# First mixer of a fused two-block kernel: where GpSimd builds its second rotation table, and where two state-space sums stand on TensorE

## The reference, cut to what matters

```python
z = hn @ hy_w_in[i]
y_a = rwkv7_time_mix(z[..., :RWKV_COLS], ...)
y_b = s5_ssm(z[..., RWKV_COLS:], ...)
y_mix = jnp.concatenate([y_a, y_b], axis=-1) @ hy_w_out[i]

def s5_ssm(u, lam_re, lam_im, ...):
    lam_bar = jnp.exp(lam * dt)
    bu = jnp.einsum('gpi,btgi->btgp', b_bar, ug)
    _, states = lax.associative_scan(combine, (lam_bar, bu), axis=1)
    y = jnp.real(jnp.einsum('gip,btgp->btgi', c_mat, states))
    y = y + d_skip * ug
    ...

def rwkv7_recurrence(r, decay, k, v, kk, a):
    def step(state, inp):
        s_kk = jnp.einsum('bhvk,bhk->bhv', state, kk_t)
        state = state * w_t - s_kk[..., None] * (kk_t * a_t) + v_t[..., None] * k_t
        return state, jnp.einsum('bhvk,bhk->bhv', state, r_t)
```

## Time and profile before

| | us |
|---|---|
| median of 3 runs | 2951.21 |
| lowest and highest | 2950.44, 2955.02 |
| the profiled execution | 2949.55 |
| its span | 2947.7 |
| first mixer's part of the span that the change touches | 54 to 244 |
| TensorE busy from 109 to 190 | 51.45 of 81.00 |
| TensorE busy from 190 to 256 | 44.82 of 66.00 |
| TensorE busy over the whole span | 2784.8 (94%) |

### The profile page before, as it was taken

One profiled execution on the slowest core, in us unless ns is written; L12 is line 12 of the kernel. 1 busy time (PEld: TensorE's weight loads), 2 busy tenths in 40 slices (PEclk: granted clock), 3 DMA queues, 4 the chain that ended last, 5 costly groups with the idle time before them and its releaser, 6 DMA issues.

```text
span 2947.7 us, 44095 instructions
## 1 busy us (share of the span) xinstructions
PE 2784.8 (94%) x18634; PEld 2478.1 (84%) x18634; DVE 2129.6 (72%) x2071; ACT 1701.7 (58%) x1770; POOL 118.0 (4%) x112
## 2 busy tenths in 40 slices
PE   8558999999799999999999999999999899999999
PEld 6447899998798878888887888888887799989999
DVE  7864545556545888888888888888888666766676
ACT  6203544346554677767776777676777564445543
POOL 5541000000000000000000000000000000000000
PEclk9888999999899999999999999999999999999999
DMA  6002435553243999899999999999999545544453
GB/s 225 30 2 73 133 126 172 185 172 116 72 161 143 352 347 359 340 354 343 354 342 349 353 354 355 344 351 350 349 356 349 215 145 168 183 132 144 158 186 129
DMA packets 238003, 690.42 MB, mean 234 GB/s; under 512 B 10608, under 2 KB 169456, under 8 KB 178416
## 3 DMA queue, kind: packets, MB, share of 16 engines
q1 hardware_dynamic: 235728, 685.52, 64.6%
q10 hardware_dynamic: 2080, 2.10, 0.2%
HBM read 686.53 MB, written 1.05 MB: 233 GB/s over the span
## 4 chain that ended last, share of the span: by engine, by line
PE 70%; DVE 9%; DMA 8%; issue 5%; ACT 4%; POOLq 2%; POOL 2%; DVEq 1%; ACTq 0%; SPq 0%
PE ps L800 20%; PE ps L802 20%; PE ps L801 20%; DMA ring<-moe 7%; DVE w_lo L3463 2%; DVE more_lo L3463 2%; PE ps L1633 1%; PE ps L860 1%; ACT arena L1766 1%; PE ps L1685 1%; DVE w_lo L1817 1%; DMA ring<-w_in 1%; PE ps L1082 1%; ACT w_hi L1801 1%; DVE mix L2588 1%
## 5 line engine op out<-in xcount | busy, mean ns | idle before, releaser
L1817 DVE TENSOR_TENSOR w_lo<-ring,w_hi 128x1024 fp32r<-128x1024 f32 x362 | 446.8, 1247 | 354.4 <-ACT w_hi L1801 353.2
L1801 ACT ACTIVATE w_hi<-ring 128x1024 fp32r<-128x1024 f32 x362 | 381.1, 1058 | 424.7 <-PE ps L802 403.9
L800 PE MATMUL ps<-x_hi,w_hi 128*128 128x256 f32 x1952 | 559.5, 287 | 13.2 <-DVE x_lo L2988 7.1
L801 PE MATMUL ps<-x_lo,w_hi 128*128 128x256 f32 x1952 | 553.7, 284 | 0.0
L802 PE MATMUL ps<-x_hi,w_lo 128*128 128x256 f32 x1952 | 553.6, 284 | 0.0
L1769 ACT ACTIVATE w_hi<-ring 128x2048 fp32r<-128x2048 f32 x232 | 445.3, 1920 | 181.8 <-DMA ring<-moe 169.6
L3463 DVE TENSOR_TENSOR w_lo<-ring,w_hi 128x2048 fp32r<-128x2048 f32 x232 | 523.4, 2286 | 16.1 <-ACT w_hi L1769 14.6
L800 PEld LDWEIGHTS ps<-x_hi,w_hi 128*128 128x128 f32 x1952 | 375.5, 192 | 21.7 <-issue 13.7
L801 PEld LDWEIGHTS ps<-x_lo,w_hi 128*128 128x128 f32 x1952 | 375.8, 193 | 0.3
L802 PEld LDWEIGHTS ps<-x_hi,w_lo 128*128 128x128 f32 x1952 | 375.7, 192 | 0.0
L1769 ACT ACTIVATE more_hi<-ring 128x2048 fp32r<-128x2048 f32 x115 | 220.7, 1919 | 133.2 <-DMA ring<-moe 127.7
(11 more groups left out here) (392 smaller groups left out, 5034.0 us busy)
## 6 DMA issues: line engine op xcount, KB each, us to landing
ring<-moe SPq DMA_DIRECT2D x347, 1024.0 KB, 6.7
more_raw<-moe SPq DMA_DIRECT2D x115, 1024.0 KB, 6.9
ring<-ffn_w_up SPq DMA_DIRECT2D x44, 1024.0 KB, 5.1
ring<-ffn_w_down SPq DMA_DIRECT2D x22, 1024.0 KB, 4.9
ring<-xa_w_kv SPq DMA_DIRECT2D x16, 1024.0 KB, 5.4
ring<-w_in SPq DMA_DIRECT2D x16, 1024.0 KB, 6.8
ring<-da_w_qkv SPq DMA_DIRECT2D x12, 1024.0 KB, 5.2
ring<-ff_w_gate SPq DMA_DIRECT2D x11, 1024.0 KB, 5.3
```

What stands on the lines that cost most here:

```text
L800: mm(o, lhs[0], rhs[0], start=start, stop=False)
L801: mm(o, lhs[0], rhs[1], start=False, stop=False)
L1801: nc.scalar.activation(w_hi[:, half_slot(at, half), :], ring[:, s_, half * 1024:half * 1024 + 1024], ACT.Copy).then_inc(hi_ready, 1)
L1817: nc.vector.tensor_tensor(w_lo[:, i, :], ring[:, s_, half * 1024:half * 1024 + 1024], w_hi[:, i, :], ALU.subtract).then_inc(lo_ready, 1)
```

## The change

Two places are edited, both orders of calls. On TensorE, `s5_sum(4)` moves from ahead of `level(3)` to behind it, and `s5_sum(5)` from ahead of `s5_drive(6)` and `level(4)` to behind both. On GpSimd, `table(1)` moves from behind `s5_out(0)` to ahead of it. No instruction is added or taken away, and every wait stays with its instruction.

```diff
@@ TensorE, pe_first_mixer
             s5_drive(5)
+            level(3)
             s5_sum(4)
-            level(3)
-            s5_sum(5)
             s5_drive(6)
             level(4)
+            s5_sum(5)
             s5_drive(7)
@@ GpSimd, pool_first_mixer
             table(0, s5_pair(0, 2))
+            table(1, s5_pair(0, 2))
             s5_out(0)
-            table(1, s5_pair(0, 2))
             s5_out(1)
```

## The result

The changed kernel takes 2935.73 us in the median of 6 runs (2932.87 to 2938.84). The kernel before, run beside it, takes 2950.82 (2945.98 to 2955.02). The ratio is 0.995 with a 95% interval of 0.9938 to 0.9962, so 15 us are gained, between 11 and 18. The forecast was 2936.5 with a gain of 14.7. The profiled execution takes 2933.28 with a span of 2931.5; before it was 2949.55 and 2947.7. Ratios and their intervals are given here as they are on record. They are not the quotients of the two medians, and a gain taken from the one can differ from the other by some 4 us.

The account below looks back on a forecast made before the run. Engines waiting in turn for one another in the first mixer were the winnable bound, the expert stage being full; 14.1 us from the levels plus 0.6 from the table took 2951.2 to 2936.5 us, range 2932 to 2941.

Parts of the forecast that it names:

- Level 3: TensorE's level 3 in the first mixer starts once add_level(2) is done, at 190.15 in place of 195.26.
- The cold clock: Level 3 starts at half clock after TensorE's idle time: 1.6 us extra, from 1.1 us a group over one and a half.
- The bound of 3.3: Upper bound on level 3's half-clock cost, with all three matmul groups cold: 3.3 us.
- Level 4's add and L1246: VectorE is free for level 4's add at 209.7; TensorE's next step, L1246, starts at 212.1, 14.1 us earlier.
- Behind L1246: The chain after the levels keeps its waits and lengths, so all of it moves by 14.1 us.
- Behind the mixer: Later stages, including the expert stage, keep their lengths, so the gain was taken in full through to the end.
- The early table: table(1) moved ahead of s5_out(0): saves 10.9 us late, delays VectorE some 10.2 us early; net gain 0.6 us.
- The rival of a TensorE that loses more than its slack: Early stall makes TensorE's chunks 5 to 8 exceed four microseconds of slack by some 5 us: 2941.5 us; chance 0.10.
- The open choice: Whether VectorE's L2565 form and a copy are blocked beside GpSimd; taken as blocked, otherwise 2.9 us less delay.
- The rival of the free table: VectorE wins its turns beside table 1 between 55 and 71, gaining 10.9 us in full: 2926.2 us; chance 0.12.
- The given-back: Levels' gain lost to GpSimd's late piece 5 or to later stages: within 2 us of before, 2950; chance 0.07.
- the slower rival: TensorE's clock stays half after its new idle stretch at 61 to 70: 19 us slower, 2970 us; chance 0.03.

Follow-up runs that it names:

- e4: Changed kernel with table(1) back behind s5_out(0), its temporary in a place of its own, operands waiting for table 0 only; 2932.96 us in one run.
- e1: Kernel before with only the two sums moved behind the levels, GpSimd's order as before; 2932.1 us against 2950.12, ratio 0.9951.
- e3: Changed kernel with table(1) left out, two zero-filling memsets in its place, so it computes something else; 2924.72 us in one run.
- e5: Changed kernel with table(1) behind s5_out(1), its temporary in s5_x, operands waiting for table 0 alone; 2933.01 us in one run.
- e2: Kernel before with only table(1) moved early, the sums as before; 2943.94 us against 2950.12, ratio 0.9983.
- e6: Changed kernel with s5_sum(5) put back ahead of s5_drive(6) and level(4), so only s5_sum(4) is moved; 2944.49 us in one run.
- e9: The kernel of e2 run a second time; 2949.25 us against 2948.39 for the kernel before, ratio 0.9999.
- e7: Changed kernel with s5_sum(1), s5_sum(6) and s5_sum(7) also moved behind the steps they stood ahead of; 2936.38 us against 2948.39, ratio 0.9951.
- e8: Changed kernel with add_level(2) ahead of s5_scan(4) on VectorE and sums 6 and 7 moved later; 2930.2 us against 2949.67, ratio 0.9921.

## Why the prediction was right, point by point

- **Level 3** was to start at 190.15 and did at 189.18; with the table half's 0.93 taken off that is exact. The cold clock was put at 1.6 us, and it was 3.68 - 2.08 = 1.60. That term came out by luck. I had 1.1 us a group over a group and a half, and it was 1.60 in one group: two errors that cancel. The bound of 3.3 for a wholly cold level was too low with it. Three groups at 1.60 are 4.8 us, and e4, with two and a part cold, lost 3.4.
- **Level 4's add and L1246.** Forecast 209.7 and 212.1, measured 208.82 and 211.22. The levels' share is 226.19 - 211.22 - 0.93 = 14.04 us against 14.1. That VectorE, not TensorE, would hold the last add is borne out: it follows `s5_in(6)` without a wait. At L1246 the two were to be level, and TensorE waits 0.40 us for L2939.
- **Behind L1246** the step "its steps have the same waits and lengths after the change, so all of it moves by 14.1" was wrong in its lengths. The chain from L1246 to L1257 took 13.90 us before and 11.13 after, since the sum at 218.59 and L1253 ran at full clock, behind the same wait of 3.4 us that had been followed by half clock before. So L1276 moved by 17.7 us, not 14.7. The term that I left out of the sum is the cold sum 6 and the cold L1253 behind it, 2.8 us. It goes with the order: the stretch takes 11.1 us in all five kernels that have the changed order of the sums and levels and nothing else changed behind level 2 (the changed one, e1, e3, e4, e5), and 13.9, 13.84 and 13.76 in before, e2 and e6. Only e9 is apart, old order and 11.13 us, but there L1246 itself ran cold (3.54 us), TensorE waited 1.87 us ahead of the sum, not 3.4, and L1246 started 1.8 us later than in e2. Why the clock was full in the one order and half in the other stays open.
- **Behind the mixer** "I take all of it through to the end" holds within scatter only. The identical rest took 2685.8 to 2695.5 us over the eleven kernels, and the changed kernel's 2692.9 is 1.5 longer than before's. The near hit of 15.1 measured against 14.7 forecast is thus partly luck: 17.7 at L1276, less 1.5 of the rest, in one profile.
- **The early table.** Forecast gain 0.6, trace 0.93; the split of chunk 5 was to end at 71.8 and ended at 71.50; operands at 99.9, were at 99.65; sum 0's partner `s5_out(0)` at 88.4, was at 87.95. The sum itself does not close: 11.2 less 0.76 is 10.4 us, and the text goes on with 10.2, and with 71.8 where 61.1 + 10.4 is 71.5. The trace has 10.4. TensorE's new wait was to be 9 us and was 7.93, since it was busy with chunk 4 until 62.57 and not until 61.5. Its slack held, as L1204 waits for VectorE, but it was thinner than the four: chunk 8 was copied out at 105.26, in e2 at 106.62, and VectorE reads it at 107.5. The rival of a TensorE that loses more than its slack was nearer than it looked. The open choice, whether the form of L2565 and a copy are blocked, fell as taken from the scan's row, though that row, with two SBUF inputs, bore on L2565 alone: the copy reads one. The Trainium skill's rule on the shared port ("SBUF — State Buffer", "Who interferes with whom"), by which two SBUF inputs, or a copy in a two-port mode, block against GpSimd's reads, agrees with both rows of the new trace, 2.25 and 1.99 us; that the copy was in such a mode no row shows. The rival of the free table is refuted by e3: the price is 10.5 us.
- **The given-back and the slower rival** did not come. Sum 5 waited for nothing, and the clock was back after one group. (The slower rival's price of 5.2 us a chunk should be 5.8 by its own 48 x 0.12, which makes it some 21 us slower, not 19.)

## What to carry to other kernels

An engine that executes in order should not have an instruction that waits for a third engine ahead of work that is ready; but all the waiting instructions have to be moved, since one that is left (e6) takes back nearly the whole gain, and everything that is fed by the moved instruction has to be looked at too (e7: a table that waited for the sum slid onto the scans). A block of GpSimd work that reads SBUF costs a dense VectorE about its own length (six instructions of 1.9 us, some 10 us) wherever it stands, as a wait, as late turns or as early ones. So before moving it, ask not whether GpSimd is idle in the new place but whether VectorE is, and what of GpSimd is pushed into what.

## What the runs showed of the hardware

- **Turns.** Beside GpSimd's products VectorE's instructions with both inputs in SBUF, and its copy, alternate with them one by one, also the short ones: a scan of 0.6 us takes 2.5 (9.89 for four), a copy of 0.43 takes 1.99. The price goes by the number of GpSimd instructions and their length (1.9 us each), hardly by VectorE's work. That one long VectorE instruction per turn would lose less than four short scans follows from this, but no run tried it. VectorE's instructions that read one input from PSUM pass freely. In the changed kernel L2913 keeps its 0.69 us beside a GpSimd instruction where L2556, just ahead of it, takes 1.88, and the add in e8 keeps its 1.21. So which of VectorE's instructions stand beside a table matters, and not only how dense it is.

```profile
172.31 1.88 DVE L2556 TENSOR_TENSOR s_x<-s_x 128x512 f32<-128x512 f32 x1
174.26 0.69 DVE L2913 TENSOR_TENSOR s_x<-mix,ps 128x512 f32<-128x512 f32 x1
173.78 2.62 POOL L3130 TENSOR_TENSOR s_e<-s_e,s_x 128x1024 f32<-128x1024 f32 x1
```

- **The clock is not a function of the wait.** The same idle gap of 2.35 us ahead of level 0 is followed by a granted clock of 1.00 in the changed kernel and of 0.54 in e1, and the kernel before, whose lists are e1's up to there, has 2.08 us for that group and e1 3.54; the same 10.2 us ahead of level 3 cost 1.6 us in the changed kernel and 3.4 in e4; the same 3.4 us ahead of sum 6 by half clock before and in e2, by full clock in the changed kernel and in e1. What was done earlier counts, but what exactly decides these runs don't show. The first case is scatter of 1.5 us, the second of 1.8, and the third came with the new order and is worth 2.8.
- **Scatter of identical work.** The stretch behind L1276 differs by 9.7 us from kernel to kernel, and two sets of runs of one kernel, on two chips, gave ratios of 0.9983 and 0.9999 to the kernel before. A difference under some 6 us was told here by marks in the trace, not by the median.
